# Scores of the second mixers as three float32r products, and weights turned one filler later

## The reference, cut to what matters

```python
s_c = jnp.einsum('bqgrd,bngd->bgrqn', qi, kc) * scale     # 31 compressed keys
p_c = masked_softmax(s_c - slopes * (t - c_mid), c_end <= t)
...
s_s = jnp.einsum('bqgrd,bqgmd->bqgrm', qi, ks) * scale    # selected keys
s_w = jnp.einsum('bqgrd,bkgd->bqgrk', qi, kw) * scale     # keys of the window
...
o = gs[..., 0:1] * o_c + gs[..., 1:2] * o_s + gs[..., 2:3] * o_w
```

## Time and profile before

| | |
|---|---|
| median of three runs | 3144.71 us (3144.15 to 3144.99) |
| time of the profiled execution | 3143.91 us |
| span in the profile, first to last instruction | 3142.6 us |
| TensorE busy | 3101.2 us (99%) |
| VectorE busy | 1359.0 us (43%) |
| ScalarE busy | 1220.8 us (39%) |
| GpSimd busy | 1348.1 us (43%) |
| granted TensorE clock | 0.999 of full speed |

### The profile page before, as it was taken

How to read it: one execution, slowest core, us unless ns; L and a number is a source line. 1 busy time by engine, 2 the same in 40 slices (tenths; PEclk the granted TensorE clock), 3 DMA queues, 4 the chain that set the end, 5 groups by cost and what they waited for, 6 DMA issues and landing times.

```text
span 3142.6 us, 42608 instructions
## 1 busy us (share of the span) xinstructions
PE 3101.2 (99%) x16832; PEld 2602.6 (83%) x16832; DVE 1359.0 (43%) x2491; ACT 1220.8 (39%) x2100; POOL 1348.1 (43%) x871
## 2 busy tenths in 40 slices
PE   8999999999999999999999999999999999999998
PEld 6877888898888987878888889888897778798887
DVE  7676533114330355755443304332056665363311
ACT  5456322233222345664432223322344564442221
POOL 4452444443444453462344444444534354334443
PEclk9999999999999999999999999999999999999999
DMA  4221333332333242231233332333432132223332
GB/s 163 81 68 54 91 97 101 95 114 67 98 100 101 78 142 62 74 112 44 81 91 97 98 90 88 101 94 101 119 97 88 48 101 82 80 69 100 101 95 67
DMA packets 80933, 285.15 MB, mean 91 GB/s; under 512 B 8928, under 2 KB 11360, under 8 KB 80480
## 3 DMA queue, kind: packets, MB, share of 16 engines
q1 hardware_dynamic: 79728, 278.59, 29.7%
q10 hardware_dynamic: 1008, 3.84, 0.3%
HBM read 280.30 MB, written 2.10 MB: 90 GB/s over the span
## 4 chain that ended last, share of the span: by engine, by line
PE 90%; DVE 4%; POOL 2%; issue 2%; ACT 2%; DMA 1%; ACTq 0%; DVEq 0%; POOLq 0%
PE bank L269 23%; PE bank L271 23%; PE bank L270 23%; PE bank L277 4%; PE bank L278 4%; PE bank L279 4%; POOL wlo L263 2%; PE bank L1524 2%; PE bank L1494 1%; PE bank L1508 1%; PE bank L3547 1%; PE bank L3573 1%; PE bank L603 1%; ACT whi L249 1%; DMA raw<-wstream 0%
## 5 line engine op out<-in xcount | busy, mean ns | idle before, releaser
L263 POOL TENSOR_TENSOR wlo<-raw,whi 128x256 fp32r<-128x256 f32 (+3 forms) x787 | 1229.3, 1577 | 1413.6 <-ACT whi L249 1380.7
L269 PE MATMUL bank<-hhi,whi 128*128 128x512 f32 x2080 | 821.4, 395 | 12.7 <-DVE wlo L263 11.0
L270 PE MATMUL bank<-hlo,whi 128*128 128x512 f32 x2110 | 821.9, 390 | 0.0
L271 PE MATMUL bank<-hhi,wlo 128*128 128x512 f32 x2080 | 810.6, 390 | 0.0
L249 ACT ACTIVATE whi<-raw 128x1024 fp32r<-128x1024 f32 (+2 forms) x502 | 501.7, 1031 | 362.3 <-PE bank L271 292.2
L269 PEld LDWEIGHTS bank<-hhi,whi 128*128 128x128 f32 x2080 | 391.1, 188 | 98.0 <-issue 19.3
L270 PEld LDWEIGHTS bank<-hlo,whi 128*128 128x128 f32 x2110 | 396.8, 188 | 81.2 <-issue 1.4
L271 PEld LDWEIGHTS bank<-hhi,wlo 128*128 128x128 f32 x2080 | 390.7, 188 | 82.5
L269 PE MATMUL bank<-ff_ahi,whi 128*128 128x512 f32 x660 | 256.7, 389 | 0.0
L271 PE MATMUL bank<-ff_ahi,wlo 128*128 128x512 f32 x660 | 256.7, 389 | 0.0
L270 PE MATMUL bank<-ff_alo,whi 128*128 128x512 f32 x630 | 245.1, 389 | 0.0
(11 more groups left out here) (429 smaller groups left out, 5211.7 us busy)
## 6 DMA issues: line engine op xcount, KB each, us to landing
raw<-wstream SPq DMA_DIRECT2D x508, 512.0 KB, 3.5
raw<-wstream SPq DMA_DIRECT2D x20, 256.0 KB, 2.6
xa_v<-memT ACTq DMA_DIRECT2D x2, 1024.0 KB, 4.9
outT<-x SPq DMA_DIRECT2D x4, 512.0 KB, 2.8
raw<-wstream SPq DMA_DIRECT2D x4, 420.0 KB, 4.3
x<-xT ACTq DMA_DIRECT2D x2, 512.0 KB, 7.9
x<-xT SPq DMA_DIRECT2D x2, 512.0 KB, 8.1
consts<-consts SPq DMA_DIRECT2D x1, 1004.0 KB, 7.5
```

What stands on the lines that cost most here:

```text
L263: last = g.tensor_tensor(h.lo[:, o:o + step], h.raw[:, o:o + step], h.hi[:, o:o + step].bitcast(F32), ALU.subtract)
L269: t.matmul(out, l[0], r[0], start=start, stop=False)
L270: t.matmul(out, l[0], r[1], start=False, stop=False)
L271: return t.matmul(out, l[1], r[0], start=False, stop=stop)
```

## The change

The scores of the second mixer become three float32r products (`SPLIT`): queries and keys, and the compressed keys, are split into high and low parts. ScalarE makes the high parts, VectorE the low ones (`dve_low`), both in the opening. Queries and keys are first evacuated to `k.tmp`. The low part of the keys (`klo[0]`) lies in the upper half of a buffer of the memory's keys, and is copied to a second place (`klo[1]`) by ScalarE near the end of block 2; rows from filler 136 on (block 3) read it there and wait for `klo_moved`. The squares of the memory lie in `m2_gr` now. TensorE waits for the last low parts ahead of the attention. In rows of six and more fillers, in both models' attention, the transposes (and on ScalarE the exponentials and copies) come after three fillers and not two.

```diff
+WHOLE, SPLIT = ((0, 0),), ((0, 0), (0, 1), (1, 0))
...
-    BEFORE_TURN = 2
+    def before_turn(self, fillers):
+        return 3 if fillers >= 6 else 2
...
+        if "wait" in self.units[step]:
+            t.wait_ge(*self.units[step]["wait"])
         if step in self.several:
             for h in range(heads):
-                for b in range(2):
-                    u = self.units[step + b]
-                    last = t.matmul(k.bank[b][:, h * 32:(h + 1) * 32], u["q"][h], u["k"], start=True, stop=True, skip_group_check=True)
+                for l, (qs, ks) in enumerate(SPLIT):
+                    for b in range(2):
+                        u = self.units[step + b]
+                        last = t.matmul(k.bank[b][:, h * 32:(h + 1) * 32], u["q"][qs][h], u["k"][ks], start=l == 0, stop=l == len(SPLIT) - 1,
+                                        skip_group_check=True)
...
         for n in range(len(both[0])):
-            for parts in both:
-                p, to = parts[n]
-                last = t.matmul(to, p["q"], p["k"], start=True, stop=True, skip_group_check=True)
+            passes = both[0][n][0]["passes"]
+            for l, (qs, ks) in enumerate(passes):
+                for parts in both:
+                    p, to = parts[n]
+                    last = t.matmul(to, p["q"][qs], p["k"][ks], start=l == 0, stop=l == len(passes) - 1, skip_group_check=True)
...
@@ MixerTwo.pe
+        t.wait_ge(*self.k_lo[1])
+        t.wait_ge(*self.kc_kept[0])
         self.att.pe(...)
...
@@ MixerTwo.act
             weight_hi(k, [self.uch, self.keych][kv].c + 2)
+        for n in range(4):
+            a.activation(self.qhi[:, n * T:(n + 1) * T], k.tmp[n][:, :], ACT.Copy).then_inc(self.q_hi.sem)
         weight_hi(k, self.cch[0][0].c + 2)
+        for n in range(2):
+            a.wait_ge(*self.k_kept[n])
+            a.activation(self.khi[:, n * T:(n + 1) * T], k.tmp[n][:, :], ACT.Copy).then_inc(self.k_hi.sem)
         self.act_hidden(0)
...
@@ MixerTwo.act_filler
+        a.wait_ge(*self.grch[1].done[-1])
+        for n in range(2):
+            o = slice(n * T, (n + 1) * T)
+            last = a.activation(self.klo[1][:, o], self.klo[0][:, o].bitcast(F32), ACT.Copy)
+        last.then_inc(self.klo_moved.sem)
...
@@ MixerTwo.dve
+        for n in range(4):
+            self.dve_low(n, self.q_hi[n], self.qhi, self.qlo, self.q_lo)
         for n in range(2):
             v.wait_ge(*self.keych.done[n])
-            v.tensor_tensor(self.keys[n][:, :], k.bank[4 + n][:, :], k.row[:, :], ALU.mult).then_inc(self.k_kept.sem)
+            v.wait_ge(*self.q_lo[n])
+            v.tensor_tensor(k.tmp[n][:, :], k.bank[4 + n][:, :], k.row[:, :], ALU.mult).then_inc(self.k_kept.sem)
+        for n in range(2):
+            self.dve_low(n, self.k_hi[n], self.khi, self.klo[0], self.k_lo)
         for ch in self.cch[0]:
             weight_lo(k, ch.c + 2, e=v)
         self.dve_hidden(0)
+        v.wait_ge(*self.kc_hi[0])
+        v.scalar_tensor_tensor(self.kcmp_lo[:, :], k.bank[0][:, 384:384 + DH], 0.5, self.kcmp_hi[:, :].bitcast(F32), ALU.mult,
+                               ALU.subtract).then_inc(self.kc_kept.sem)
...
+    def dve_low(self, n, hi_made, hi, lo, made):
+        v, o = self.k.nc.vector, slice(n * T, (n + 1) * T)
+        v.wait_ge(*hi_made)
+        v.tensor_tensor(lo[:, o], self.k.tmp[n][:, :], hi[:, o].bitcast(F32), ALU.subtract).then_inc(made.sem)
```

More of the change, by code:

```diff
@@ L1483, in pe_scores @@
             for h in range(heads):
-                for b in range(2):
-                    u = self.units[step + b]
-                    last = t.matmul(k.bank[b][:, h * 32:(h + 1) * 32], u["q"][h], u["k"], start=True, stop=True, skip_group_check=True)
-                    if h == heads - 1:
-                        last.then_inc(self.scores.sem)
+                for l, (qs, ks) in enumerate(SPLIT):
[3 more added lines that the diff above has]
+                                        skip_group_check=True)
+                        if h == heads - 1 and l == len(SPLIT) - 1:
+                            last.then_inc(self.scores.sem)
             return
@@ L1491, in pe_scores @@
         for n in range(len(both[0])):
-            for parts in both:
-                p, to = parts[n]
-                last = t.matmul(to, p["q"], p["k"], start=True, stop=True, skip_group_check=True)
-                if n == len(parts) - 1:
-                    last.then_inc(self.scores.sem)
+            passes = both[0][n][0]["passes"]
[3 more added lines that the diff above has]
+                    last = t.matmul(to, p["q"][qs], p["k"][ks], start=l == 0, stop=l == len(passes) - 1, skip_group_check=True)
+                    if n == len(parts) - 1 and l == len(passes) - 1:
+                        last.then_inc(self.scores.sem)
     def pe_turn(self, i):
@@ L1534, in pe @@
             for n in range(fillers):
-                if n == self.BEFORE_TURN and turn is not None:
+                if n == self.before_turn(fillers) and turn is not None:
                     if gone is not None and self.closes(gone):
@@ L2806, in __init__ @@
         self.at_keys = put.at[0]
-        self.both_keys = put("m2_ksw", 2 * T)
-        self.keys = [self.both_keys[:, n * T:(n + 1) * T] for n in range(2)]
+        self.khi = put("m2_khi", 2 * T, F32R)
         at_vr = put.at[0]
@@ L2856, in __init__ @@
         self.at_weights = put.at[0]
-        units, self.rows = [], []
+        units, self.rows, at = [], [], 0
         for qb in range(TB):
@@ L2860, in __init__ @@
                 rows = slice(DH * gi, DH * gi + DH)
-                units.append(dict(n=P, heads=4, q=[self.qT[rows, j * T + qb * P:j * T + (qb + 1) * P] for j in range(4)],
-                                  k=self.kcmp[rows, gi * 32:(gi + 1) * 32], bias=self.cbias[:, :], make_bias=(lambda step, qb=qb, gi=gi: self.make_cbias(qb, gi)),
+                units.append(dict(n=P, heads=4, q=[[x[rows, j * T + qb * P:j * T + (qb + 1) * P] for j in range(4)] for x in (self.qhi, self.qlo)],
+                                  k=[x[rows, gi * 32:(gi + 1) * 32] for x in (self.kcmp_hi, self.kcmp_lo)], bias=self.cbias[:, :], make_bias=(lambda step, qb=qb, gi=gi: self.make_cbias(qb, gi)),
                                   v=[lambda kb, gi=gi, j=j: self.vblock[gi][:, j * DH:(j + 1) * DH] for j in range(4)]))
             self.rows.append((qb, (), ()))
+            at += 8
             for js in self.JOINED.get(qb, [(j,) for j in range(4)]):
@@ L2867, in __init__ @@
                     for gi in range(2):
-                        parts = [self.score_part(qb, j, gi, branches) for j in js]
+                        moved = at >= self.MOVED
+                        parts = [self.score_part(qb, j, gi, branches, self.klo[moved]) for j in js]
                         units.append(dict(n=sum(p["n"] * len(branches) for p in parts), parts=parts))
+                        if moved:
+                            units[-1]["wait"] = self.klo_moved[0]
                     self.rows.append((qb, js, branches))
+                    at += sum(self.per_row(len(units) - 2 + gi, qb) for gi in range(2))
         self.cat_nsa = NormOutputs(k, 4, self.up[:, :], self.o_dump, self.total[:, :], lambda j: k.p2(l, "nsa_out_g", j),
@@ L2965, in pe, with score_part @@
         self.out.pe(2)
-    def score_part(self, qb, j, gi, branches):
+    def score_part(self, qb, j, gi, branches, klo):
         n, rows, o = (qb + 1) * P, slice(DH * gi, DH * gi + DH), j * T + qb * P
-        keys = self.both_keys[rows, :].rearrange("p (b t) -> p b t", b=2)[:, :, 0:n] if len(branches) == 2 else self.keys[branches[0]][rows, 0:n]
-        return dict(n=n, q=self.qT[rows, o:o + P], k=keys, slope=SLOPES[4 * gi + j], dist=self.k.c("dist", T - n, n), at=j * P,
+        both = [x[rows, :].rearrange("p (b t) -> p b t", b=2)[:, :, 0:n] if len(branches) == 2 else x[rows, branches[0] * T:branches[0] * T + n]
+                for x in (self.khi, klo)]
+        return dict(n=n, q=[x[rows, o:o + P] for x in (self.qhi, self.qlo)], k=both, passes=SPLIT, slope=SLOPES[4 * gi + j],
+                    dist=self.k.c("dist", T - n, n), at=j * P,
                     v=[lambda kb, at=br * P + gi * DH: self.vtok[:, kb * 256 + at:kb * 256 + at + DH] for br in branches])
@@ L2978, in per_unit, with per_row @@
         qb, js, _ = self.rows[step // 2]
-        return (7, 4, 3, 3 + (step % 4 == 3))[qb] if js else 4
+        return self.per_row(step, qb) if js else 4
+    def per_row(self, step, qb):
+        return (7, 4, 3, 3 + (step % 4 == 3))[qb]
     def windows(self, u, n):
@@ L3193, in dve @@
         for c, ch in enumerate(self.qch):
-            run(keep_dve(k, ch, lambda m: self.qT[:, (2 * c + m) * T:(2 * c + m + 1) * T], DH ** -0.5, self.q_kept))
+            run(keep_dve(k, ch, lambda m: k.tmp[2 * c + m][:, :], DH ** -0.5, self.q_kept))
         for kv in range(2):
```

27 lines of the change are left out of this document (17 added, 10 removed).

## The result

The changed kernel takes 3152.2 us (median of 11 runs, 3151.6 to 3152.6), the kernel before on the same chip 3144.7 us (11 runs, 3143.9 to 3146.0). The ratio is 1.0024, 95% interval 1.0015 to 1.0032: slower by 7.5 us. I had said 3144.2 with a range up to 3152.0, so the measured time lies 0.2 us outside it. The profiled execution took 3151.8 us, 3150.5 of it span.

The account below looks back on a forecast made before the run. TensorE, busy 99% of the span, was taken as the bound. Opening +4.0, scores -3.5 and turns -1.0 summed to -0.5 us, a median of 3144.2 us; range 3137.5 to 3152.

Parts of the forecast that it names:

- q low parts: 1116.2 to 1118.7: Opening, VectorE: four q subtractions in a row at a spacing of about 0.6 us, done by 1118.7.
- the opening's term of the sum: Opening of each second mixer: 2.0 us a layer added, ends 1.4 and 2.8, with a TensorE stop of 1.8 us.
- Scores: Second mixers' score steps: three float32r products instead of float32 save 1.7 us a layer, 3.5 in all.
- Turns: Transposes one filler later: the 0.46 us stop at the first ones goes, about 1.0 us in all with the restart.
- the total of stops between 1280 and 1300: Late in block 2, a sign in the profile after: TensorE's stops there stay about the same in total.
- Loads: TensorE's float32r products: weight loads take no time in line, since 256-column products follow each other in 0.12 us.
- rival 4: Score steps: weight loads stand in line with products at 0.112 us a load; 10 us more, 3155; chance 3%.
- rival 2: Score steps: row halves no longer run side by side in float32r; 38 us more, 3183; chance 6%.
- Key copies: End of block 2: two ScalarE copies of 0.63 us cost nothing; without idle cover 1.2 us a layer.
- the copies of turned weights: ScalarE in block 3: copies behind a later transpose have 2.4 us of cover for 0.7.
- Rival 3: Opening: handovers cost 0.3 us more each or fetches crowd, 5 to 6 us a layer, 3152; chance 11%.
- The fetches: Opening: raw-slot loads for later weight halves move by the same 2.2 us, less what less crowded fetching gains.

Follow-up runs that it names:

- run 9: The changed kernel, but in each opening GpSimd makes only 256 of 1024 columns of four weight low parts, the rest left out: 3145.4 us, ratio 1.0001.
- run 8: The changed kernel with own buffers for q and keys, and q lows 2 and 3 moved behind the first two weight low parts: 3148.9 us, ratio 1.0015.
- run 10: The kernel before, with GpSimd making only 256 of 1024 columns of four weight low parts in each opening: 3142.5 us, ratio 0.9993.
- run 2: The changed kernel with the transposes after two fillers everywhere, as before (the scores alone): 3153.8 us, ratio 1.0029.
- Run 5: The changed kernel with q and key lows (own buffers) behind the first hidden layer, and block 2's transposes back after two fillers: 3142.9 us, ratio 0.9998.
- run 3: The changed kernel with q and keys in own buffers and all their lows behind the first hidden layer on VectorE: 3143.1 us, ratio 0.9996.
- run 7: The changed kernel with q and key lows (own buffers) behind the second hidden layer, and block 2's transposes back after two fillers: 3141.3 us, ratio 0.9991.
- run 4: The changed kernel with q and key lows (own buffers) behind the first hidden layer, and transposes after two fillers everywhere: 3144.5 us, ratio 1.0001.

## Why the prediction was wrong

**The failed step** is the first item of the opening's list, "q low parts: 1116.2 to 1118.7", with "four VectorE instructions in a row keep a spacing of about 0.6". Because of it the opening's term of the sum was mis-sized (2.0 us a layer, ends 1.4 and 2.8; measured 5.3 to 5.5), by two things:

- *GpSimd holds VectorE up.* The row that gave the 0.6 is m_q<-bank,row: one of its inputs is in PSUM. The other, L1317, has both on chip in SBUF, but no instruction of GpSimd runs beside it: all 105 take 691 to 694 ns. The lows read two SBUF tiles while GpSimd works until 1120.34. The row I should have looked for stands in both kernels: two kinds with two SBUF inputs, of the same 128x512 (min/median/max in ns, from the trace after; run 9 shows it to be the cause in the opening):
```profile
L562 DVE TENSOR_TENSOR tmp<-tmp,tmp x45: 691/693/2844, 606.8 to 3106.0; 128x512 f32<-128x512 f32 x45
L1315 DVE SCALAR_TENSOR_TENSOR tmp<-tmp,tmp x110: 691/693/2611, 371.4 to 3015.9; 128x512 f32<-128x512 f32 x110
```
  The median is that of the quiet ones. The maximum is the price beside GpSimd. The page of before has their group means too, 1101 and 1193 ns, far from 692.
  The Trainium skill (SBUF — State Buffer, "Who interferes with whom") says that a VectorE instruction with two SBUF inputs contends with a GpSimd instruction that reads SBUF; it calls the pair of ports that they share an exclusive lock, and has the order of issue decide who blocks. The trace agrees: 2.89 us for the low that began inside a GpSimd instruction, 0.68 for the lows without one. I had not weighed that rule, and it spoke against the change.
- *The clock.* With a stop of 3.84 us came 3.4 us at half clock in both layers, with one of 2.65 (run 8) likewise, with one of 2.27 (run 9) in one layer of two. Where all 3.4 us fall on work they cost 1.4 (run 9). My sum had a stop with no price behind it.

How the 5.3 to 5.5 us divide: run 9 less run 10 in the layer without the half clock is 30.76 - 28.25 = 2.5, the opening's cost without either of the two, inside the ends that I gave. The half clock is 1.4 in the first layer; in the second 2.7 of its 3.4 us fell on work, 1.1 as an estimate. The remaining 1.6 to 1.7 is a difference: GpSimd's full-length instructions cost the changed kernel 2.4 us a layer beside the clock (34.58 less 30.76 and 1.4, 34.25 less 30.76 and 1.1), and the kernel before 0.7 to 0.8 (before less run 10). The hold itself is 2.6 us on VectorE (1.07 and 2.89 for two instructions of 0.68).

**Scores**, 1.7 us a layer: the steps are right to 0.03 us. Alone they gave 1.1 (run 2). I had let VectorE's chain late in block 2 take up one compressed and one 384 step, so that 0.34 us of cost would vanish there; instead its stops grew by 0.63 (2.99 for 2.36). Steps that came out 0.2 us a layer cheaper than forecast made up for some of it.

**Turns**, 0.5 a layer: the stop went, but the gain came back as later stops in block 2. I had said that "what the transposes gain is waited for there", yet took that as no loss; it is one of 0.7 with the old scores. The two edits together reach 1.9 a layer (2.2 forecast), though alone they give 1.1 and nothing; that was not foreseen. I had also said that the total of stops between 1280 and 1300 would stay about the same, and it grew from 2.36 to 3.17. Run 5 shows that the sum of the late stops is not set by the place of block 2's transposes. The last of them ends 4.85 us after an exponential that waits for VectorE; which work of VectorE ahead of that sets its moment stays open.

**Loads** in line with the products: rival 4 did not occur, nor rival 2. **Key copies** and the copies of turned weights: no stop that the kernel before does not have. **Rival 3** had the right place and, by luck, the right time (5 to 6 a layer, 3152), but the wrong mechanism: in the chain of waits of this stretch the handovers between ScalarE and VectorE are 0.02 to 0.03 us each, not 0.3 more. The piece "issue" of 2.21 lies in the middle of the second low:
```profile
1116.44 0.53 ACT m_qhi L3094
1116.97 0.02 issue
1117.00 1.60 DVE m_qlo L3267 x2
1118.60 2.21 issue
1120.80 0.14 DVE m_qlo L3267
```
The fetches are not it either: no stop of TensorE that names a transfer appeared.

## What to carry to other kernels

Before pricing a VectorE instruction from a row, see whether its inputs are both in SBUF and whether GpSimd is busy at the place it goes to; read the maximum of such a group, not its mean or median. Work whose result is wanted 10 us later goes behind what TensorE waits for next, even if the engine seems idle now: here that order was worth 9 us (run 3), more than I expected of the whole change. Before putting a stop of TensorE of some microseconds into a sum, allow for the clock behind it: here up to 1.4 us more.

## What was not expected of the hardware

A 128x512 subtraction took 0.68 us on VectorE alone and 2.89 us beside a 2.67 us GpSimd instruction (1.87 to 2.88 in run 3). Instructions of this size with both inputs in SBUF that began while GpSimd made a low part ended 0.55 us after it: the lows here, and all 64 of L562 and L1315 in the kernel before. TensorE's granted clock was 0.5 for 3.4 us behind stops of 2.3 to 3.8 us, or from shortly before their end (6.8 us once, in run 2). It also fell behind two stops of 0.89 and 0.73 (run 7) and of 1.10 and 0.99 (run 4), and stayed at 1.00 behind 2.27 (run 9, second layer) and behind 0.48, 1.01 and 0.38 (run 3). What decides between the two isn't shown here.
